# An up-sum three beats behind its dot product: product of gelu and gate at the end of the second beat

## What is computed

```python
def chunk(args):
    h_c, e_c, g_c = args
    a = jnp.einsum('cd,ced->ce', h_c.astype(jnp.float32), u[e_c].astype(jnp.float32))
    act = jax.nn.gelu(a, approximate=False) * g_c
    return jnp.einsum('ce,ced->cd', act, v[e_c].astype(jnp.float32))
```

## Time and profile before

| what | value |
|---|---|
| median of 3 runs | 3934.88 us (3934.09 to 3949.5) |
| the profiled execution's own time | 3945.4 us |
| its span, first to last instruction | 3942.6 us |
| busy: PE, DVE, ACT, POOL | 3030.5, 2347.3, 903.3, 1143.1 us |
| mean granted TensorE clock | 0.831 of 2.4 GHz |
| DMA moved | 1263.86 MB, of it 1073.81 MB by POOL's queue of gathers |
| gathers, first and last issue | 811.8 and 3912.9 us |
| DMA to landing, gathers | 5.3 / 10.2 / 16.1 us (min, median, max) |

### The profile page before, as it was taken

How to read it: one execution, slowest core, us unless ns; L and a number is a source line. 1 busy time by engine, 2 the same in 40 slices (tenths; PEclk the granted TensorE clock), 3 DMA queues, 4 the chain that set the end, 5 groups by cost and what they waited for, 6 DMA issues and landing times. The chain is left out here.

```text
span 3942.6 us, 50876 instructions
## 1 busy us (share of the span) xinstructions
PE 3030.5 (77%) x18686; PEld 1573.7 (40%) x18686; DVE 2347.3 (60%) x6030; ACT 903.3 (23%) x2462; POOL 1143.1 (29%) x1029
## 2 busy tenths in 40 slices
PE   5975596836797766989899875979899876666666
PEld 4853395711354311543455522634455521111111
DVE  6547744477445677457545578457645577655554
ACT  2113332112112111127321112127321111111111
POOL 0000000034333444233323332323333344444443
PEclk8997698977898877987899986979999977766666
DMA  5520002379999999989999997988999999999998
GB/s 216 184 75 0 5 4 74 116 309 403 392 361 376 417 404 410 394 333 365 377 403 371 360 406 275 403 308 313 389 400 383 360 403 392 415 419 414 419 420 351
DMA packets 207061, 1263.86 MB, mean 321 GB/s; under 512 B 25748, under 2 KB 28948, under 8 KB 72356
## 3 DMA queue, kind: packets, MB, share of 16 engines
q0 software_dynamic: 147456, 1073.81, 67.8%
q1 hardware_dynamic: 59368, 186.95, 12.8%
HBM read 1256.17 MB, written 4.46 MB: 320 GB/s over the span
## 5 line engine op out<-in xcount | busy, mean ns | idle before, releaser
L243 POOL DMA_INDIRECT held_z<-in_experts,held_expert x512 | 572.2, 1118 | 1253.6 <-PE held_acc L263 885.2
L263 PE MATMUL held_acc<-held_z,held_diag 64*64 64x512 f32 x4096 | 691.4, 772 | 276.0 <-ACT held_diag L289 254.1
L263 PE MATMUL held_acc<-held_pair,held_diag 64*64 64x512 f32 x4096 | 687.8, 765 | 249.7 <-ACT held_diag L289 248.2
L243 POOL DMA_INDIRECT held_pair<-in_experts,held_expert x512 | 567.1, 1108 | 1024.2 <-PE held_acc L263 954.5
L309 DVE CUSTOM_DVE_ANT_0 held_z<-held_z,held_hrow 128x1024 f32<-128x1024 f32 x512 | 625.4, 1224 | 388.0 <-DMA held_z<-in_experts,held_expert 384.7
L309 DVE CUSTOM_DVE_ANT_0 held_pair<-held_pair,held_hrow 128x1024 f32<-128x1024 f32 x512 | 625.1, 1224 | 373.6 <-DMA held_pair<-in_experts,held_expert 365.2
L289 ACT ACTIVATE held_diag<-held_bands,held_weight 128x64 f32<-128x64 f32 x1024 | 347.7, 340 | 1470.5 <-DVE held_weight L304 1470.0
L263 PEld LDWEIGHTS held_acc<-held_z,held_diag 64*64 64x64 f32 x4096 | 136.9, 156 | 696.0 <-ACT held_diag L289 557.8
L263 PEld LDWEIGHTS held_acc<-held_pair,held_diag 64*64 64x64 f32 x4096 | 133.7, 155 | 674.2 <-ACT held_diag L289 576.9
L282 ACT ACTIVATE held_bent<-held_dot 128x2 f32<-128x2 f32 x512 | 104.0, 203 | 715.9 <-DVE held_dot L309 699.6
L1951 PE MATMUL c_ps<-held_hT,c_w 128*128 128x256 f32 x640 | 152.9, 394 | 0.0
(11 more groups left out here) (501 smaller groups left out, 3972.2 us busy)
## 6 DMA issues: line engine op xcount, KB each, us to landing
pgh_w<-in_w_in SPq DMA_DIRECT2D x38, 512.0 KB, 8.0
p2h_w<-in_w_in SPq DMA_DIRECT2D x36, 512.0 KB, 7.8
p_raw<-in_w_in SPq DMA_DIRECT2D x34, 512.0 KB, 3.6
p_w_ada<-in_w_ada SPq DMA_DIRECT2D x16, 1024.0 KB, 6.0
c_w<-in_w_query SPq DMA_DIRECT2D x20, 512.0 KB, 4.8
held_z<-in_w_in SPq DMA_DIRECT2D x20, 512.0 KB, 7.9
c_w<-in_w_peer_q SPq DMA_DIRECT2D x20, 512.0 KB, 7.9
ada_w<-in_w_ada SPq DMA_DIRECT2D x4, 2048.0 KB, 18.8
```

Source lines behind the costliest of these rows:

```text
L243: pool.indirect_dma_start(self.pair[m % BUFS], None, self.layers[t // TT][0], bass.IndirectOffsetOnAxis(ap=self.expert[:, t % TT, s:s + 1] ...
L263: last = pe.matmul(self.sum_of(i)[to * BAND:(to + 1) * BAND], diag[band, :], up[band, turn * WIDE:(turn + 1) * WIDE], start=s == 0, stop=s ...
```

## The change

`WEIGH_AT` becomes 2, and with it `DIAG_AT` 2, `UP_AT` 3 and `AHEAD` 5. In `dve` the product moves behind the dot product of its beat. The number of instructions of each kind stays.

```diff
 BENT_AT = GROUP
-WEIGH_AT = GROUP + 1
+WEIGH_AT = GROUP
 DIAG_AT = WEIGH_AT
 UP_AT = DIAG_AT + 1
 AHEAD = BUFS - UP_AT
@@
     def dve(self, dve, n):
-        g, s = divmod(n - WEIGH_AT, GROUP)
-        if s == 0 and 0 <= g < SLOTS // GROUP:
-            t, q = divmod(g, NJ // GROUP)
-            at = slice(q * GROUP, (q + 1) * GROUP)
-            dve.wait_ge(self.bent_made, g + 1)
-            dve.tensor_tensor(self.weight[:, t % 2, at], self.bent[:, t % 2, at], self.gate[:, t % TT, at], ALU.mult).then_inc(self.weighed, 1)
         if n < SLOTS:
...
             if n % GROUP == GROUP - 1:
                 ins.then_inc(self.dotted, 1)
+        g, s = divmod(n - WEIGH_AT, GROUP)
+        if s == 0 and 0 <= g < SLOTS // GROUP:
+            t, q = divmod(g, NJ // GROUP)
+            at = slice(q * GROUP, (q + 1) * GROUP)
+            dve.wait_ge(self.bent_made, g + 1)
+            dve.tensor_tensor(self.weight[:, t % 2, at], self.bent[:, t % 2, at], self.gate[:, t % TT, at], ALU.mult).then_inc(self.weighed, 1)
```

## The result

The changed kernel takes 3998.35 us (median of 4 runs, 3994.11 to 4000.99), beside 3941.54 us for the kernel before (4 runs): a ratio of 1.0138, 95% interval 1.0121 to 1.0154. It is slower, by more than the forecast and its range allowed (3948, at most 3982). The profiled execution took 3997.73 us, 52 us more than that of before.

What follows compares the result with a forecast made beforehand. It took DMA to bound the last stretch, DMA and PE the projection, and PE with DVE's order the query stages. Terms 12 + 3 + 4 + 6 - 3 - 7 - 2 = +13 us gave 3948 on the median, range 3910 to 3982.

Steps and rivals of the forecast that it cites:

- absorption: First and last hosted query stages: DMA lands gathers already issued while PE waits, leaving 4 of 14 and 3 of 12 us.
- (a): Hosted query stages: one more dot product (1.15 us) delays the product an up-sum needs; +4, +12 and +3 us.
- paid in full: Hosted query stages with none of PE's added waits absorbed: 12 + 12 + 14 = 38 us.
- (b): Two attentions: product waits more for gelu, +9 us each, less 12 us credited for landing waits; net +6 us.
- the drain: Attentions: 1.38 us extra per table switch would add 44 us; left out of the sum, given 1 in 100.
- (c): First query stage of the second mixer: extra time for slots to land cuts landing waits; -3 us.
- (d): Hand-overs from unfilled to full stretches: -2.5 us for each that DMA limits, three counted; -7 us.
- (e): Odd slot's diagonal comes sooner: 0 in the last stretch, -2 us in top-16 stages, bounds 0 and 4 us.
- slower in full: Whole kernel: nothing absorbed, landing waits off the path; +56 us, some 3990; chance 0.32 including the half case.
- Faster: Whole kernel: later dot products free DVE of landing waits; -32 us, some 3903, or 3919 at half strength; chance 0.16.
- the way by a higher rate of the last stretch: Unhosted last stretch: more requests in flight lift DMA from 415 towards 435 GB/s, gaining 27 us; 3 in 100.

Runs made afterwards that it cites:

- late_product_q1: Kernel before, plus a needless VectorE instruction of a dot product's length ahead of every product of gelu and gate in the first hosted query stage; 3964.11 us, 1.0052.
- late_product_q3: Kernel before, plus a needless VectorE instruction of a dot product's length ahead of every product of gelu and gate in the last query stage; 3961.69 us, 1.0055.
- filled_hosted_only: Changed kernel, plus six needless TensorE matmuls in each step with a piece, only in the three query stages with hosted beats; 3977.72 us, 1.0083.
- change_filled_waits: Changed kernel, plus six needless TensorE matmuls ahead of the up-sums in each step with a piece, the unhosted first query stage included; 3997.32 us, 1.0127.
- lag_only: Kernel before with the lag a beat shorter (five slots in flight), the product still ahead of its beat's dot product; 3962.82 us, 1.0048.
- hosted_first: Kernel before with VectorE's hosted beats moved ahead of the top-16 piece in the chunk steps of the query stages; 3940.16 us, 0.9984.

## Why the prediction was wrong, by its own steps

**The step that failed is the absorption in (a)**: "what PE loses, DMA uses to land gathers already issued ... of 12 I take 3", and the same for Q1. The waits themselves were sized right: 14, 12 and 12 us forecast for Q1, Q2 and Q3, 12.9, 11.9 and 11.2 measured, single ones of up to 3.7 as foreseen, and over the prediction's whole stretch (2192:2363 of the changed kernel) 33.0 us in 15, where it had about 30 in 15 or more. But Q1 and Q3 paid in full, as Q2 did, and late_product_q1 and late_product_q3 show it without the rest of the change: +21.4 and +19.6 us, with no more than 4.9 and 3.5 given back behind. The reason is read from the kernel's order and was not tested by itself: when PE waits, its up-sums free no buffer and POOL has nothing to issue (its waits for PE in Q2 grew from 73 to 100 us, and the DMA share fell to 0.85), and the stretch behind has as many slots to fetch as ever. The share of 0.98 that I leaned on said that DMA was busy, not that it was late. The waits of DVE for landing would not have told it either: in the chunk steps of Q1 they were 1.7 us before and 20.1 us in late_product_q3, which has the same code there, and the two stages took 134.1 and 134.3 us.

**The term that is missing from (a)** is the clock: 16.5 us of chunk matmuls by the page of the profile, 24.6 us with all of PE's matmuls in the three stages, and some 20 us that filled_hosted_only won back. With 38 forecast for "paid in full", the query stages cost 59. Against the 19 us that (a) had in the sum, some 19 were missing for absorption and some 21 for the clock.

**(b) The attention** came out with the other sign. The product waits for the gelu more often than I said (20 + 21 times, 37 us, in place of 30 near 1 us), yet A1 is 7.6 us shorter and A2 level; by size, +6 was forecast and -8 came. Over the whole of A1 landing waits fell from 15.6 to 7.7 us, but that this shortened it is not shown. The granted clock over A1 was 0.80 before and 0.91 in the change, and PE's busy time there 11 us less. A1 scatters with that clock: with before's code in it five kernels show 143.0 to 152.5 (mean 146.9), with the change's five show 140.5 to 142.3 (mean 141.3) and change_filled_waits 152.7, so the 7.6 us are rather 5 or 6. In before's code the clock is 0.79 in the longest (152.5) and 0.87 in the shortest (143.0); in the change's it is 0.90 to 0.94 in the five and 0.83 in the sixth. So the gain in A1 goes with TensorE's clock, and the prediction has no term for it; what sets the clock there stays open. The mechanism of (b) is real nonetheless: lag_only, without the dot product ahead, pays 12 and 16 us for it. That table load and gelu follow without the drain that the Trainium skill (ScalarE: Activation LUTs, What ACT_TABLE_LOAD costs) adds held after too: in A1 of the changed kernel a load begins at 1814.30 us, straight behind the activation before it, and its gelu at 1815.59, and the change's 41 waits have a mean of 0.9 us, near the 0.95 worked out without it.

**(c)** The landing waits of Q2, 16.6 us in its chunk steps, are gone, and it brought nothing: DVE now waits for PE instead, 69.6 us before its copies in place of 26.6. **(d)** No hand-over gave 2.5 us that can be told from noise; -7 was forecast, and outside the query stages and attentions the change moved +0.3 us in sum. In lag_only the end is 7 us shorter than before, so something of the kind may exist, but it was not followed up. **(e)** The order on ACT is as said, and worth 0 in the last stretch, inside its bounds.

**The rival "slower in full"**, +56 or 3990 at a chance of 0.32, fits nearly to the microsecond (the medians differ by 56.8), but that is luck: its sum was right by two errors of opposite sign, 18 us for attentions that came out 8 us shorter, and some 21 us of clock that it lacked. What it had right is that nothing of (a) is absorbed. Of *Faster*, the way by a higher rate of the last stretch (27 us) did not come: 417 GB/s with five slots in flight, beside 415 with four.

Three experiments missed their numbers in a way that bears on the reading: hosted_first (3900 to 3920 expected, 3940 measured), for which the cause stays open; lag_only's attentions (5 to 10 us each expected, 12 and 16 measured); and change_filled_waits (3975 to 3985 expected, 3997 measured), for the first query stage and A1.

## What to carry to other kernels

A wait that is lengthened on the engine that sets a stage's pace was paid in full here in three stages of three, at DMA shares of 0.96 and 0.97 before. Neither the share nor the waits for landing told whether it would be absorbed; adding one needless instruction ahead of the one that is waited for, in one stage, did, and a control with the same instruction behind it ruled out the load itself. Cut the stretches that you compare at the same instructions: two windows laid by eye gave 0.95 and 0.99 for stages that had 0.97 and 0.96. Add to a lengthened TensorE wait what its next matmuls cost at the lower clock, here about half to two thirds as much again as the waits. The right place for a small instruction that others wait for differs from stage to stage. And what else stands ahead of it can matter more than the lag: with the piece of 2.7 us out of the way the change cost nothing, though on the kernel before the same move brought only 0.2%.

## What the runs showed of the hardware that was not expected

After a wait of 3.47 us PE's next eight up-sum matmuls took 1.99 us in place of 1.09 and its next sixteen chunk matmuls 5.78 in place of 3.72; the granted clock was 0.50 over the first and 0.64 over the second. With 2.76 us of needless matmuls in such a wait the eight and the sixteen took 1.09 and 3.72 us, and the kernel ran 20 us faster for doing more. And in the last stretch the granted clock was 0.76 in place of 0.66 and PE's busy time 336 in place of 401 us for the same work, at no difference in its length: there TensorE's clock is worth nothing.
